# Attention in a one-core Trainium2 kernel: the product of weights and values two steps behind the scores instead of one

## The chip, the cores and the metric

The kernel runs on one core of a Trainium2 chip. The metric is the device time of one execution in microseconds (us); the median of 3 runs is given, and each profile is that of one execution.

## What is computed

The reference is two blocks of layers on 1024 tokens of width 1024. The first is a hybrid mixer with a feed-forward part; the change doesn't touch it. The second has two layers: one with causal attention over 12 heads and one with a linear recurrence, and both with an attention over 256 memory tokens with 4 heads. What matters here:

```
def causal_attention(q, k, v):            # 12 heads, 1024 tokens, q and k 96 wide, v 64 wide
    scale = 1.0 / math.sqrt(d)
    sc = einsum('bqhd,bkhd->bhqk', q_blk, k) * scale
    sc = where(k_pos <= q_pos, sc, -inf)
    p = softmax(sc, axis=-1)
    return einsum('bhqk,bkhd->bqhd', p, v)

def memory_attention(q, mem_k, mem_v):    # 4 heads of 64, 256 memory tokens
    sc = einsum('bshd,bmhd->bhsm', q, mem_k) / math.sqrt(HEAD_DIM)
    p = softmax(sc, axis=-1)
    return einsum('bhsm,bmhd->bshd', p, mem_v)
```

## The kernel before

The kernel is written with explicit semaphores. Each engine has its own list of instructions and runs it in order; where data passes from one engine to another, the reader waits for a count. The function `attention` (from line 3325) is used twice: for the token attention (`causal`, U = 12 heads) and for the memory attention of the second layer (U = 4 heads). The memory attention of the first layer is other code and isn't touched.

The scores are kept transposed: keys on the partitions, queries along the row. A step is one block of 128 keys (`s`) against one half of the queries, 512 of them (`t`). A head u of the token attention has 12 steps: 4 for the first half (t = 0, s = 0 to 3), 8 for the second (t = 1, s = 0 to 7). Blocks on the diagonal and right of it are shorter, 512, 384, 256 and 128 queries, and get a mask product. `mine` is the list of a head's steps. In the memory attention a head has 4 steps, two for each half, all of 512 queries.

For each step n:

- TensorE forms the scores (line 3557, f32, two passes), called S(n) here, into one of two PSUM banks, `ps[:, 4 + n % 2]`. It first waits until the exponential of step n-2 has read that bank (line 3555). On the diagonal a mask product follows (line 3561).
- ScalarE takes the exponential into one of four buffers `pr[:, n % 4]` (line 3602), after the product of step n-4 has read that buffer.
- TensorE multiplies the values with these weights (`weigh(n)`, lines 3482 to 3492, f32, two passes), called W(n), accumulated over the steps of a half in bank 6 + t. It waits for the exponential of step n. The values carry columns of ones, so the sums of the weights come out with it.
- After the last step of a half, VectorE takes the reciprocal of the sums and multiplies (`normalise`, lines 3635 and 3636). It waits for W of that half's last step: W(3) for the first half, W(11) for the second.

To subtract a maximum, the kernel forms for the next head, u + 1, ahead of time the scores a second time in rounded form (`maxima(u + 1, b)`, b = 0 to 7, lines 3508 and 3511), called M(b): each 128 queries against all keys up to them, up to 1024. They go to two pairs of PSUM banks in turn. M(0) waits for the rounded q of that head, which VectorE casts (line 3654); M(b) waits until the content two jobs earlier has been read, which for b from 2 on is the reduction of b-2 on VectorE (`take_maxima`, line 3622). After the eight, `to_rows` (line 3523) turns the maxima by a product with the identity, VectorE negates them (line 3666), and SyncE writes the row to memory and loads it as a 97th row of q by two DMAs (lines 3430 and 3435). The scores of the next head wait for the second DMA.

The order on TensorE around one head: S(0), S(1), the transposition of the next head's values (`turn_values`, line 4197), W(0), then for n from 2: S(n), W(n-1), M(n-2), as long as there are M; at the end `to_rows` and W(11). Then come the projections of K and Q of the head after the next (`project`, line 288 with `latents`), then the next head. On VectorE: reductions 0 and 1, normalise of the first half, reductions 2 to 7, the negated row, normalise of the second half, then rotation and cast of q for the head after the next. ScalarE copies the projections and the values between its exponentials (lines 4202 to 4208). In the memory attention there is nothing between the steps; the maxima of the head after the next follow the head.

Of the kernel before, what the change touches and what calls it, by code (L numbers as in the profile page):

```python
# [157 lines left out]
def build(nc, a):  # L158
    ctx = ExitStack()
    with ctx:  # L160
# [3164 lines left out]
        def attention(iters, U, dq, keys_n, scale, q_of, k_of, v_of, out_of, sfx, rounded, project=None, gating=None):  # L3325
# [61 lines left out]
            with ExitStack() as scope:  # L3387
# [20 lines left out]
                with nc.Block() as block:  # L3408
# [48 lines left out]
                    @block.tensor  # L3457
                    def _(pe):
                        def body(i):
                            reached = {"act": -1, "dve": -1}  # L3460

                            def reads_of(e, value):

                                if value > reached[e]:
                                    reached[e] = value
                                    pe.wait_ge(free[e].sem, val(i, after[e][-1], value))

                            def pair_of(job):

                                j = at[job]  # L3470
                                if j >= 2 or i is not None:
                                    before = (j - 2) % J
                                    for e in readers[jobs[before][0]]:
                                        per = after[e][-1]
                                        value = b_e[e] + after[e][before] - (per if j < 2 else 0)
                                        reads_of(e, value)
                                return pair[j % 2]

                            def evacuated(e, job):
                                reads_of(e, b_e[e] + after[e][at[job]])  # L3480

                            def weigh(n):
                                u, t, s = steps[n]
                                lo, hi = span(t, s)
                                g = 2 * u + t

                                pe.wait_ge(act_p.sem, val(i, len(steps), b_p + n + 1))
                                if s == 0 and (g >= 2 or i is not None):

                                    pe.wait_ge(dve_o.sem, val(i, 2 * U, b_do + g - 1))  # L3490
                                nc.tensor.matmul(ps[:, 6 + t, lo - HALF * t:HALF], v_of(u, s), pr[:, n % 4, 0:hi - lo],  # L3491
                                                 start=(s == 0), stop=(s == last(t))).then_inc(pe_o.sem, 1)

                            def turn_values(u):
                                evacuated("act", ("K", u, 0))
                                project.turn(pair_of(("V", u, 0)))

                            def maxima(u, b):

                                if causal and b == 0:  # L3500
                                    evacuated("act", ("Q", u, 0))
                                    evacuated("dve", ("Q", u, 0))
                                o = pair_of(("A", u, b))
                                if causal:
                                    n_keys = (b + 1) * P
                                    for lo in range(0, n_keys, HALF):
                                        hi = min(lo + HALF, n_keys)
                                        nc.tensor.matmul(o[:, lo:hi], rounded(u)[0][:, b * P:(b + 1) * P],
                                                         rounded(u)[1][:, lo:hi], start=True,
                                                         stop=(hi != n_keys))  # L3510
                                    mm = nc.tensor.matmul(o[:, b * P:n_keys], masks_r[:, 0], masks_r[:, 1],
                                                          start=False, stop=True)
                                else:
                                    for j in range(4):
                                        mm = nc.tensor.matmul(
                                            o[:, j * MEM:(j + 1) * MEM],
                                            rounded(u)[0][:, (4 * b + j) * P:(4 * b + j + 1) * P],
                                            rounded(u)[1], start=True, stop=True)
                                mm.then_inc(pe_done.sem, 1)

                            def to_rows(u):
                                evacuated("dve", ("A", u, CH - 1))
                                nc.tensor.matmul(pair_of(("R", u, 0))[0:CH, 0:P], mx[:, u % 2], ident, start=True,
                                                 stop=True).then_inc(pe_done.sem, 1)

                            for kind, u in seq:
                                if kind == "P":
                                    project(pe, i, u, pair_of, s0)
                                if kind == "V":
                                    turn_values(u)  # L3530
                                if kind == "A":
                                    for b in range(CH if causal else 2):
                                        maxima(u, b)
                                if kind == "R" and causal:
                                    if u == 0:
                                        to_rows(u)
                                elif kind == "R":
                                    evacuated("dve", ("A", u, 1))
                                    o = pair_of(("R", u, 0))
                                    for c in range(CH):  # L3540
                                        mm = nc.tensor.matmul(o[dq:dq + 1, c * P:(c + 1) * P], mx[:, u % 2, c:c + 1],
                                                              ident, start=True, stop=True)
                                    mm.then_inc(pe_done.sem, 1)
                                if kind == "S":
                                    evacuated("dve", ("R", u, 0))
                                    if causal:
                                        evacuated("act", ("V", u, 0))
                                        pe.wait_ge(*row_in.at(16 * (u + 1)))
                                    mine = [n for n, st in enumerate(steps) if st[0] == u]
                                    for n in mine:  # L3550
                                        _, t, s = steps[n]
                                        lo, hi = span(t, s)
                                        if n >= 2 or i is not None:

                                            pe.wait_ge(act_p.sem, val(i, len(steps), b_p + n - 1))
                                        diag = causal and s >= 4 * t
                                        mm = nc.tensor.matmul(ps[:, 4 + n % 2, 0:hi - lo],  # L3557
                                                              k_of(u)[0:dq + 1, s * P:(s + 1) * P],
                                                              q_of(u)[0:dq + 1, lo:hi], start=True, stop=not diag)
                                        if diag:  # L3560
                                            mm = nc.tensor.matmul(ps[:, 4 + n % 2, 0:P], masks_r[:, 0], masks_r[:, 2],  # L3561
                                                                  start=False, stop=True)
                                        mm.then_inc(pe_s.sem, 1)
                                        if causal and u + 1 < U and n - mine[0] == 1:

                                            turn_values(u + 1)
                                        if n > mine[0]:
                                            weigh(n - 1)
                                        if causal and u + 1 < U:
                                            if 2 <= n - mine[0] < 2 + CH:  # L3570
                                                maxima(u + 1, n - mine[0] - 2)
                                    if causal and u + 1 < U:
                                        to_rows(u + 1)
                                    weigh(mine[-1])
                        looped(pe, body)

                    @block.scalar
# [1096 lines left out]
```

## Time and profile before

| | |
|---|---|
| median of 3 runs | 3223.11 us (3221.61 to 3223.95) |
| profiled execution | 3219.17 us, its span 3217.4 us |
| granted TensorE clock, mean over the span | 0.948 |
| TensorE, matmul (PE) | 2929.7 us, 91% |
| VectorE (DVE) | 1504.3 us, 47% |
| ScalarE (ACT) | 1082.7 us, 34% |
| GpSimd (POOL) | 925.9 us, 29% |

The span is what the profiler sees from the first to the last instruction; the execution's own time is a little longer. Busy times of engines overlap. An idle time in a row stands before the instruction it names, with what ended it behind the arrow. The token attention lies at 2323 to 2685 us of the span, the memory attention of the second layer at 3027 to 3086 us.

### The profile page before, as it was taken

Reading aid. Unit: us, or ns where it says so; the run is one execution under the profiler, and the core shown is the slowest. Engines: PE = TensorE matmul, PEld = TensorE weight load, DVE = VectorE, ACT = ScalarE, POOL = GpSimd, SP = SyncE. Lnnn points to the kernel's source line nnn. Section 1 sums busy time; section 2 is a strip of 40 time slices with the busy share of each in tenths; the row PEclk is TensorE's granted clock in tenths of the full one; section 3 lists DMA queues with packets and bytes.
Section 4 is the critical chain, followed back from the end, with each engine's and each line's share of the span. In section 5 each row is a group of like instructions: output and inputs, shape, how many; then the busy total and the mean of one; then the engine's idle time right before and its main releaser. Section 6 shows DMA issues by size and latency. Waiting matters only on the chain. (4 is left out here: it accounts for less than half of the span.)

```text
span 3217.4 us, 34284 instructions
## 1 busy us (share of the span) xinstructions
PE 2929.7 (91%) x14130; PEld 2188.3 (68%) x14130; DVE 1504.3 (47%) x1551; ACT 1082.7 (34%) x1462; POOL 925.9 (29%) x487
## 2 busy tenths in 40 slices
PE   5799999999988889799999999999699998899886
PEld 4677777777766567578887787776455556667565
DVE  4272012243525442565554345343366663639555
ACT  4242122212135123433333444345234341347312
POOL 3241111214332122345544345331112111233110
PEclk8899999999999989899999999999799999899897
DMA  7111124652133352212223453312200001121201
GB/s 291 33 60 53 53 73 149 197 183 79 53 101 123 105 196 62 76 53 79 79 82 102 150 186 122 114 55 73 105 14 20 14 20 72 59 79 33 95 14 53
DMA packets 86173, 286.52 MB, mean 89 GB/s; under 512 B 8849, under 2 KB 13217, under 8 KB 84865
## 3 DMA queue, kind: packets, MB, share of 16 engines
q1 hardware_dynamic: 86018, 284.33, 26.3%
q8 instruction: 112, 1.84, 0.2%
q14 instruction: 43, 0.35, 0.0%
HBM read 219.70 MB, written 64.59 MB: 88 GB/s over the span
## 5 line engine op out<-in xcount | busy, mean ns | idle before, releaser
L280 POOL TENSOR_TENSOR w_lo_sb<-raw_w_sb,w_hi_sb 128x1024 fp32r<-128x1024 f32 x195 | 492.2, 2525 | 1585.0 <-ACT w_hi_sb L271 1584.8
L288 PE MATMUL ps<-h_hi_sb,w_hi_sb 128*128 128x512 f32 x720 | 298.3, 414 | 23.2 <-PEq L910 19.6
L271 ACT ACTIVATE w_hi_sb<-raw_w_sb 128x1024 fp32r<-128x1024 f32 x195 | 205.2, 1052 | 247.9 <-PE ps L288 191.7
L288 PE MATMUL ps<-h_lo_sb,w_hi_sb 128*128 128x512 f32 x720 | 287.5, 399 | 0.0
L288 PE MATMUL ps<-h_hi_sb,w_lo_sb 128*128 128x512 f32 x720 | 244.7, 400 | 0.0
L288 PE MATMUL ps<-merged_parts_hi_sb,w_hi_sb 128*128 128x512 f32 x472 | 192.7, 408 | 18.3 <-PEq L535 7.4
L288 PE MATMUL ps<-z_lo,w_hi_sb 128*128 128x512 f32 x512 | 205.2, 401 | 0.0
L288 PE MATMUL ps<-merged_parts_lo_sb,w_hi_sb 128*128 128x512 f32 x472 | 188.0, 398 | 0.0
L288 PEld LDWEIGHTS ps<-h_hi_sb,w_hi_sb 128*128 128x128 f32 x720 | 137.3, 191 | 67.3 <-issue 34.3
L288 PE MATMUL ps<-merged_parts_hi_sb,w_lo_sb 128*128 128x512 f32 x472 | 178.0, 399 | 0.0
L288 PE MATMUL ps<-z_hi,w_hi_sb 128*128 128x512 f32 x384 | 161.8, 421 | 14.9 <-PEq L910 5.6
L288 PEld LDWEIGHTS ps<-h_hi_sb,w_lo_sb 128*128 128x128 f32 x720 | 137.3, 191 | 33.8
L288 PEld LDWEIGHTS ps<-h_lo_sb,w_hi_sb 128*128 128x128 f32 x720 | 137.5, 191 | 30.6 <-issue 1.0
L288 PE MATMUL ps<-hid_hi_sb,w_hi_sb 128*128 128x512 f32 x352 | 140.5, 399 | 12.9 <-DVE hid_lo_sb L3183 12.9
L3183 DVE TENSOR_TENSOR hid_lo_sb<-ffn_hidden_sb,hid_hi_sb 128x512 fp32r<-128x512 f32 x88 | 85.6, 980 | 127.6 <-ACT hid_hi_sb L3154 127.5
L288 PE MATMUL ps<-hid_lo_sb,w_hi_sb 128*128 128x512 f32 x352 | 140.5, 399 | 0.0
L288 PE MATMUL ps<-hid_hi_sb,w_lo_sb 128*128 128x512 f32 x352 | 139.9, 397 | 0.0
L3557 PE MATMUL ps<-qh_sb,kh_sb 97*128 97x512 f32 (+3 forms) x288 | 123.2, 514 | 13.6 <-DMA qh_sb<-att_rows 11.0
L288 PE MATMUL ps<-z_hi,w_lo_sb 128*128 128x512 f32 x384 | 134.1, 403 | 0.0
L3491 PE MATMUL ps<-att_p_t_sb,vh_sb 128*128 128x512 f32 (+3 forms) x288 | 124.5, 514 | 8.8 <-ACT att_p_t_sb L3602 8.8
L3602 ACT ACTIVATE att_p_t_sb<-ps 128x512 f32<-128x512 f32 (+2 forms) x144 | 69.3, 488 | 175.1 <-PE ps L3561 104.6
L3003 POOL TENSOR_TENSOR w_lo_sb<-ffn_weight_sums_sb,w_hi_sb 128x512 fp32r<-128x512 f32 x72 | 106.8, 1487 | 54.0 <-ACT w_hi_sb L2957 53.7
(627 smaller groups left out, 6391.6 us busy)
## 6 DMA issues: line engine op xcount, KB each, us to landing
raw_w_sb<-in_w SPq DMA_DIRECT2D x231, 512.0 KB, 3.6
ada_late_sb<-in_ada SPq DMA_DIRECT2D x32, 512.0 KB, 3.7
inbox_sb<-gates_out SPq DMA_DIRECT2D x24, 512.0 KB, 4.0
ffn_hidden_out<-ffn_hidden_box_sb SPq DMA_DIRECT2D x22, 512.0 KB, 6.3
ffn_hidden_sb<-ffn_hidden_out SPq DMA_DIRECT2D x22, 512.0 KB, 4.6
ada_w_sb<-in_ada SPq DMA_DIRECT2D x16, 512.0 KB, 8.7
gates_out<-outbox_sb SPq DMA_DIRECT2D x16, 512.0 KB, 2.6
inbox_sb<-sums_out SPq DMA_DIRECT2D x16, 512.0 KB, 4.6
```

Source lines behind the costliest of these rows:

```text
L271: nc.scalar.activation(w_hi[:, n % RING].rearrange("p t m -> p (t m)"), raw_w[:, n % RAW], ACT.Copy).then_inc(w_rounded.sem, 1)
L280: nc.gpsimd.tensor_tensor(w_lo[:, n % RING].rearrange("p t m -> p (t m)"), raw_w[:, n % RAW], flat_hi, ALU.subtract).then_inc(w_split.sem, 1)
L288: mm = nc.tensor.matmul(o, wt, xs, start=start and part == 0 and xs is x_hi, stop=stop and part == 1, skip_group_check=again)
L3003: nc.gpsimd.tensor_tensor(flat4(half_slot(w_lo, j)), weight_of(g, j), flat4(half_slot(w_hi, j)).bitcast(F32), ALU.subtract).then_inc(split ...
L3183: nc.vector.tensor_tensor(hs[1][:, j % RING], source(j), hs[0][:, j % RING].bitcast(F32), ALU.subtract).then_inc(hid_s.sem, 1)
L3491: nc.tensor.matmul(ps[:, 6 + t, lo - HALF * t:HALF], v_of(u, s), pr[:, n % 4, 0:hi - lo], start=(s == 0), stop=(s == last(t))).then_inc(pe ...
L3557: mm = nc.tensor.matmul(ps[:, 4 + n % 2, 0:hi - lo], k_of(u)[0:dq + 1, s * P:(s + 1) * P], q_of(u)[0:dq + 1, lo:hi], start=True, stop=not ...
L3602: nc.scalar.activation(pr[:, n % 4, 0:hi - lo], ps[:, 4 + n % 2, 0:hi - lo], ACT.Exp, scale=scale).then_inc(act_p.sem, 1)
```

## The change

`weigh` of a step stands two steps behind the scores instead of one. Within a head, W(n-2) is issued behind S(n), from the third step on, and both W(n-2) and W(n-1) of the last step follow at the end, behind `to_rows`. It holds for both uses of `attention`. The other engines' lists, the buffers and the waits' conditions are unchanged.

```diff
@@ -3564,13 +3564,14 @@
                                         if causal and u + 1 < U and n - mine[0] == 1:
 
                                             turn_values(u + 1)
-                                        if n > mine[0]:
-                                            weigh(n - 1)
+                                        if n > mine[1]:
+                                            weigh(n - 2)
                                         if causal and u + 1 < U:
                                             if 2 <= n - mine[0] < 2 + CH:
                                                 maxima(u + 1, n - mine[0] - 2)
                                     if causal and u + 1 < U:
                                         to_rows(u + 1)
+                                    weigh(mine[-2])
                                     weigh(mine[-1])
                         looped(pe, body)
```

## Rows read from the trace of the kernel before

**Rows 1.** The page, busy time of each engine, share of the span, instructions.
```profile
PE 2929.7 (91%) x14130; PEld 2188.3 (68%) x14130; DVE 1504.3 (47%) x1551; ACT 1082.7 (34%) x1462; POOL 925.9 (29%) x487
```

**Rows 2.** Grouped by line, PE, 2355 to 2660: busy, mean ns; idle before, releaser.
```profile
L3491 PE MATMUL ps<-att_p_t_sb,vh_sb 128*128 128x512 f32 (+1 forms) x240 | 102.4, 508 | 8.8 <-ACT att_p_t_sb L3602 8.8
...
L3508 PE MATMUL ps<-k_rounded_sb,q_rounded_sb 96*128 96x512 f32 (+2 forms) x120 | 54.5, 508 | 16.3 <-DVE q_rounded_sb L3654 9.6 <-DVE att_max_t_sb L3622 6.6
```

**Rows 3.** Windows, one head: length, busy of each engine, granted clock, DMA share.
```profile
2386.20:2417.40 31.20, 28.68 (x118) 17.13 (x117) 20.73 (x17) 12.79 (x20) 3.04 (x1) 1.00 0.06 18
```

**Rows 4.** Order of time, PE, one head: start, duration, instruction, idle before it.
```profile
2389.80 1.13 PE L3491 MATMUL ps<-att_p_t_sb,vh_sb 128*128 128x512 f32 x2 [0.89 <-ACT att_p_t_sb L3602]
...
2391.26 0.86 PE L3491 MATMUL ps<-att_p_t_sb,vh_sb 128*128 128x384 f32 x2
2393.09 0.30 PE L3508 MATMUL ps<-k_rounded_sb,q_rounded_sb 96*128 96x128 f32 x1 [0.97 <-DVE q_rounded_sb L3654]
...
2395.22 0.39 PE L3491 MATMUL ps<-att_p_t_sb,vh_sb 128*128 128x128 f32 x2
2395.36 0.42 PE L3508 MATMUL ps<-k_rounded_sb,q_rounded_sb 96*128 96x384 f32 x1
...
2395.70 1.08 PE L3557 MATMUL ps<-qh_sb,kh_sb 97*128 97x512 f32 x2
2396.61 1.02 PE L3491 MATMUL ps<-att_p_t_sb,vh_sb 128*128 128x512 f32 x2
...
2397.77 1.08 PE L3557 MATMUL ps<-qh_sb,kh_sb 97*128 97x512 f32 x2
2398.68 1.02 PE L3491 MATMUL ps<-att_p_t_sb,vh_sb 128*128 128x512 f32 x2
2400.37 0.56 PE L3508 MATMUL ps<-k_rounded_sb,q_rounded_sb 96*128 96x512 f32 x2 [0.66 <-DVE att_max_t_sb L3622]
...
2408.15 0.86 PE L3491 MATMUL ps<-att_p_t_sb,vh_sb 128*128 128x384 f32 x2
2408.85 0.39 PE L3557 MATMUL ps<-qh_sb,kh_sb 97*128 97x128 f32 x2
```

**Rows 5.** Order of time, DVE, the same head.
```profile
2390.22 2.73 DVE L3654 CAST q_rounded_sb<-qh_sb 32x1024 fp32r<-32x1024 f32 x1
...
2395.65 3.36 DVE L3635 RECIPROCAL att_rec_t_sb<-ps 64x512 f32<-64x512 f32 x1 [0.71 <-PE ps L3491]
...
2399.76 2.10 DVE L3622 TENSOR_REDUCE att_max_t_sb<-ps 128x1 f32<-128x384 f32 x3
```

**Rows 6.** Order of time, PE, the first scores of the last head.
```profile
2662.40 1.10 PE L3557 MATMUL ps<-qh_sb,kh_sb 97*128 97x512 f32 x2 [2.57 <-issue]
```

**Rows 7.** Order of time, DVE, memory attention: first row of maxima, last head's first reciprocal.
```profile
3042.57 1.22 DVE L3669 TENSOR_SCALAR lru_qm_sb<-ps 1x1024 f32<-1x1024 f32 x1 [0.51 <-PE ps L3541]
...
3077.72 3.35 DVE L3635 RECIPROCAL att_rec_m_sb<-ps 64x512 f32<-64x512 f32 x1 [0.71 <-PE ps L3491]
```

**Rows 8.** Windows, PE alone, 8 us from an idle stretch's start: length, busy, clock, DMA.
```profile
27.50:35.50 8.00, 3.68 (x44) 1.00 0.82 277
187.80:195.80 8.00, 6.17 (x67) 1.00 0.20 68
254.30:262.30 8.00, 6.19 (x58) 0.79 0.20 66
291.40:299.40 8.00, 5.55 (x17) 0.79 0.29 97
...
1362.10:1370.10 8.00, 6.80 (x30) 1.00 0.68 255
...
2154.70:2162.70 8.00, 5.45 (x20) 0.79 0.28 99
2659.80:2667.80 8.00, 5.43 (x14) 0.79 0.01 2
```

## The prediction

> **What bounds the kernel now.** I read the page first: TensorE (PE) is busy 91% of the span, so a wait of PE costs time and a wait of another engine does not [rows 1]. Then I grouped the instructions by line over the ten full heads of the token attention, 2355 to 2660 us. That shows where PE stands still and who ends it: 8.8 us ahead of the products with the values, ended by ScalarE's exponentials; and 16.3 us ahead of the score products for the maxima of the next head, all of it ended by VectorE (DVE), 9.6 us by its cast of the rounded q and 6.6 us by its reduction [rows 2]. One head takes 31.2 us at a granted clock of 1.00 [rows 3]. Last I read one head in order of time, PE beside DVE. I call a score product S, the product of weights and values W, a product for the maxima of the next head M. A head has S0 to S11, W0 to W11 and M0 to M7. The order before is S(n), W(n-1), M(n-2).
>
> The reader should see three stops of PE in each head [rows 4]: 0.89 us ahead of W0, 0.97 us ahead of M0, 0.66 us ahead of M4; the rest is back to back. M0 waits for DVE's cast, which starts at 2390.22 and takes 2.73 us: it ends at 2392.95, M0 starts at 2393.09. M4 waits for the third reduction. DVE works through a fixed list: reductions 0 and 1, then the reciprocal and the product of the head's first half, then reductions 2 to 7. The reciprocal waits for W3, the last product of the first half; it starts at 2395.65, takes 3.36 us, and the reductions start at 2399.76 [rows 5]. From the start of the reciprocal to M4 it is 2400.37 - 2395.65 = 4.72 us. So in this part of the head the path runs W3, reciprocal, product, reduction, M4, and PE fills only a part of it with M2, S5, W4, M3, S6, W5.
>
> **What the change moves.** W(n-2) stands behind S(n), and the last two W stand at the head's end, behind the transposition of the maxima. No instruction is added or removed, on any engine, and no DMA. What each move costs, in order:
>
> *The stop ahead of W0.* W0 waits for exponential 0. In the new order S2 stands first, but S2 writes the buffer that exponential 0 reads, so it waits for the same event. The 0.89 us stay. The gain that the change seems to offer, cover for the exponentials, is already there in the rest of the head: no other W of the full heads shows an idle PE, since 8.8 us is ten heads by 0.88 [rows 2]. I cost the gain at nothing; what hides the exponential at present is the S that stands between.
>
> *The stop ahead of M0.* Its end is set by DVE's cast and stays. W1 ran in front of it (2391.26) and now runs behind M0, behind S3. It has 384 columns; such a W takes 2408.85 - 2408.15 = 0.70 us [rows 4]. So the stop grows from 0.97 to about 1.67 us.
>
> *W3, and DVE behind it.* Between M0 and W3 there now stand also W1 (0.70), M2 (at most 2395.70 - 2395.36 = 0.34 us; I take 0.3) and S5 (2396.61 - 2395.70 = 0.91) [rows 4]. W3 ends 1.9 us later. What waits in DVE's list behind it is the reciprocal and, queued behind that, all reductions from 2 on, and PE waits for reduction 2 at M4. M4 starts 1.9 us later.
>
> *The stop ahead of M4.* W5 (0.9 us, as S5; it has the same 512 columns) was done before M4 and is now done after it. So M4 comes 1.9 us later with 0.9 us less behind it: 2.8 us a head. Check from the other side: between W3 and M4 PE loses M2, S5 and W5 of its filling, 0.3 + 0.91 + 0.9 = 2.1 us, so this stop grows from 0.66 to about 2.8 us; with 0.70 at M0 that is 2.8 again. Behind M4 PE is back to back, before and after, so nothing is won back.
>
> *Count.* Ten heads have both stops: 28 us. The first head, which lies ahead of that stretch, finds its cast long done and has no stop ahead of M0, but the same list of DVE: 2.1 us. The twelfth has no M. Together 30.1 us. The bounds: 2.5 a head if M2 costs nothing, 3.1 if each of the moved products leaves a tenth of a us more between itself and its neighbour than the rows show; 27 to 33 us.
>
> *The end of a head.* The transposition of the maxima stands ahead of W10 now, so the row of maxima leaves for its two DMAs about 0.5 us earlier (W10 has 256 columns, against 0.70 us for 384). Those DMAs are hidden behind the projections of the head after the next, except for the last head, where PE stops 2.57 us [rows 6]: -0.5 us. The queue of SyncE is moved past nothing else; GpSimd waits for the second half's product only, whose place stays.
>
> *Memory attention.* Four heads of four steps. W1 now stands behind S3, about 0.9 us later, and DVE's reciprocal behind it. In the first and third head DVE stood only 0.51 us idle before the next head's row of maxima [rows 7], so 0.4 us each comes through; in the last head the chain from 3077.72 on is DVE's alone, two reciprocals and two products, and the next stage waits for it: 0.9 us. Together +1.7 us. Less than nothing here would need a stop at the last W, and PE shows none to speak of; more would need the half clock, so 0 to 4 us.
>
> Sum without the clock: 30.1 - 0.5 + 1.7 = 31.3 us.
>
> **The clock.** A stop of PE can also cost speed afterwards. In this trace I looked up the single idle stretches of PE inside dense work and the granted clock over the 8 us from their start [rows 8]. With about 1.2 us idle (8 less 6.80 busy) the clock stays at 1.00. With about 1.8 us it stays once (187.80) and falls once (254.30); over all six stretches between 1.76 and 1.96 us three were followed by a fall. With 2.2 to 2.6 us (291.40, 2154.70, 2659.80 and two more) it fell in five of six; the sixth (27.50) kept 1.00. A mean of 0.79 over 8 us is 8 x 0.21 = 1.7 us of full-speed work lost, at the lower of the two levels, 1.2 instead of 2.4 GHz, until the clock rose again. The new stop ahead of M4, 2.8 us, is at or above the longest of these, so I take 5/6 x 11 heads x 1.7 = 15.6 us. The stop ahead of M0 becomes 1.67 us with the 0.89 us one close before it; its nearest rows are those at 1.8 us. I take one head in three: 3.4 x 1.7 = 5.8 us. Bounds: nothing, or 21 falls by 1.7 = 36 us. I take 21.4 us, since the rows at 2.5 us are the nearest to the larger stop.
>
> The Trainium skill ("TensorE: Matmul & The Clock Gate", section "HAM oscillation — how this bites in real kernels") warns only of idle gaps longer than the two reckoned here. By that rule no head would lose any clock and the time would be that of the rival without the clock, below; the trace does not agree, since 2.5 us was enough for it five times.
>
> Sum: 31.3 + 21.4 = 52.7 us. The profiled execution has a span of 3217.4 and a time of 3219.17 us, so it would take 3271.9; it lies 3.9 us under the median of the three runs, 3223.11, and from that the sum gives 3275.8. I say 3274.
>
> **Rivals.**
> *The stops without the clock.* Only the M0 and M4 mechanism: 3223.1 + 27 to 38 = 3250 to 3261. For it: two gaps of 0.89 and 0.97 us in every head left the clock at 1.00 [rows 3], and one of 2.2 us did. Against it: rows 8.
> *The clock falls at both stops in every head.* 31.3 + 36 = 67, and a few falls that last twice as long: 3287 to 3305. For it: the two stops ahead of M0 add to 2.5 us within some 4 us. Against it: the stop at M0 alone, 1.67 us, is shorter than any after which the clock fell.
> *Faster.* The place is the wait of W0 for exponential 0: if it went into the cover of S2, and the stop at M4 were set by the buffers rather than by DVE's list, ten heads would gain 0.88, some 9 us: 3214. The point from which it decides: exponential 0 has to be done before S2's turn, and reduction 2 has to start before W3 ends. Neither the list of DVE nor S2's buffer allows it.
> *Nothing changes.* The two orders would be worth the same if PE's stops merely changed places: 3217 to 3229. It would need M4 not to wait for W3's reciprocal; the 0.66 us in each head say it does.
>
> **Chances.** The forecast with clock (3262 to 3286) 0.50; without clock 0.20; both stops 0.20; some other slower way, such as memory attention at half clock throughout, 0.02; faster 0.04; no change 0.04. The range has to take in most of the first three: I reach down to 3248, below the case without clock, and up to 3294, half of the case with both. That leaves out about 0.18. What a measurement of this kernel can tell from no change is about 0.2%, 6.4 us. Faster 0.04, within 0.04, slower 0.92.
>
> **What would show it.** In the changed kernel's page DVE stays at 1504 us of busy time and PE's grows only by what runs at half clock. Grouped by line over the same ten heads, the idle time ahead of the maxima's score products grows from 16.3 to about 45 us, some 28 of it ended by DVE's reduction and 16 to 17 by the cast; the 8.8 us that ScalarE ends stay, but stand ahead of S2. In order of time the reciprocal starts 1.9 us later after M0. The granted clock in a head's stretch falls to between 0.90 and 0.97. I am wrong if M4's stop stays near 0.7 us (then DVE was not what it waits for), or if it is 2.8 us and the clock stays at 1.00 (then only the step on the clock fails).

## The result and the profile after

The changed kernel takes 3295.99 us (median of 6 runs, 3285.35 to 3297.74), the kernel before in the same series 3222.36 (6 runs, 3217.72 to 3227.60). The ratio is 1.022, with a 95% interval of 1.021 to 1.023: slower by 2.2%, 73.6 us by the medians. The forecast was 3274 us, 1.6%. The ratio applied to the 3223.11 us from which the forecast was made gives 3294.3, at the very top of its range of 3248 to 3294; the median itself lies 2 us above it. One execution below, the profiled one of the first filling experiment, was disturbed as a whole (12811.73 us) and is left out of that kernel's time.

The profiled execution has a span of 3294.3 us, 76.9 more than before. The work is the same, PE's busy time is longer. First the page, busy time of each engine, against [rows 1]:

```profile
PE 2976.1 (90%) x14130; PEld 2210.9 (67%) x14130; DVE 1503.7 (46%) x1551; ACT 1082.7 (33%) x1462; POOL 925.1 (28%) x487
```

Where the time came from, by stretches of the span. From the kernel before, the token attention and the memory attention (length; busy of PE, its weight loads, DVE, ACT, POOL; granted clock; DMA share, GB/s):

```profile
2322.80:2681.40 358.60, 329.67 (x1302) 193.86 (x1302) 226.01 (x186) 137.28 (x222) 60.88 (x22) 0.99 0.05 15
3031.60:3086.50 54.90, 45.85 (x130) 20.13 (x128) 42.53 (x26) 9.55 (x16) 0.00 (x0) 0.82 0.02 7
```

The same two of the changed kernel:

```profile
2327.80:2754.60 426.80, 369.41 (x1302) 211.51 (x1302) 226.15 (x186) 137.19 (x222) 60.88 (x22) 0.89 0.04 13
3104.80:3163.60 58.80, 47.09 (x130) 21.10 (x128) 42.55 (x26) 9.55 (x16) 0.00 (x0) 0.80 0.01 5
```

The token attention is 68.2 us longer, the memory attention 3.9. The remaining 5 us lie ahead of both, in code that the change doesn't touch. That part ends at 2322.8 us before, at 2327.8 after, and in the experiments below between 2320.7 and 2335; so it differs from one execution to the next, and I draw nothing from it. I compare stretches and heads within the attention. Heads 1 to 9 take 31.16 to 31.17 us from start to start in the kernel before, and 31.14 to 31.19 in an execution of another kernel below that keeps their order.

PE grouped by line over the ten full heads of the changed kernel (2363 to 2736 us; busy, mean ns; idle before, releaser), against [rows 2]:

```profile
L3557 PE MATMUL ps<-qh_sb,kh_sb 97*128 97x512 f32 (+1 forms) x243 | 122.1, 592 | 11.1 <-ACT att_p_t_sb L3603 8.8 <-issue 2.3
L3491 PE MATMUL ps<-att_p_t_sb,vh_sb 128*128 128x512 f32 (+1 forms) x240 | 114.1, 567 | 0.0
L3508 PE MATMUL ps<-k_rounded_sb,q_rounded_sb 96*128 96x512 f32 (+2 forms) x120 | 65.6, 605 | 43.0 <-DVE att_max_t_sb L3623 26.8 <-DVE q_rounded_sb L3655 16.1
```

The 8.8 us that ScalarE's exponentials end stand now ahead of the scores instead of the product with the values, and are the same 8.8. The idle time ahead of the maxima's products grew from 16.3 to 43.0 us. And the means grew: 567 ns for the product with the values where [rows 2] has 508. That is the clock, as the stretches below show.

One head in order of time, PE (start, duration, instruction, idle before it), against [rows 4]:

```profile
2367.28 0.70 PE L3557 MATMUL ps<-qh_sb,kh_sb 97*128 97x256 f32 x2 [0.89 <-ACT att_p_t_sb L3603]
...
2370.56 0.30 PE L3508 MATMUL ps<-k_rounded_sb,q_rounded_sb 96*128 96x128 f32 x1 [1.61 <-DVE q_rounded_sb L3655]
...
2372.00 1.91 PE L3557 MATMUL ps<-qh_sb,kh_sb 97*128 97x512 f32 x2
...
2376.18 0.39 PE L3491 MATMUL ps<-att_p_t_sb,vh_sb 128*128 128x128 f32 x2
...
2381.33 0.56 PE L3508 MATMUL ps<-k_rounded_sb,q_rounded_sb 96*128 96x512 f32 x2 [2.69 <-DVE att_max_t_sb L3623]
...
2383.07 1.91 PE L3491 MATMUL ps<-att_p_t_sb,vh_sb 128*128 128x512 f32 x2
```

And DVE beside it, against [rows 5]:

```profile
2367.69 2.72 DVE L3655 CAST q_rounded_sb<-qh_sb 32x1024 fp32r<-32x1024 f32 x1
...
2376.60 3.35 DVE L3636 RECIPROCAL att_rec_t_sb<-ps 64x512 f32<-64x512 f32 x1 [3.98 <-PE ps L3491]
...
2380.72 2.11 DVE L3623 TENSOR_REDUCE att_max_t_sb<-ps 128x1 f32<-128x384 f32 x3
...
2412.11 3.36 DVE L3636 RECIPROCAL att_rec_t_sb<-ps 64x512 f32<-64x512 f32 x1 [2.30 <-PE ps L3491]
```

The reader should see three things. The three stops are 0.89, 1.61 and 2.69 us where they were 0.89, 0.97 and 0.66. DVE stands idle 3.98 us ahead of the reciprocal, waiting for W3, where it stood 0.71: the late W3 starts the chain late, and the chain itself is unchanged, 2376.60 to 2381.33 = 4.73 us (4.72 before). Part of the 3.98 us is the low clock between M0 and W3. The last row is of the next head, where the clock stayed up behind M0 at 2407.74: there DVE stands idle 2.30 us, and the reciprocal starts 4.37 us behind M0 where it started 2.56 before, so 1.8 us later by the order alone. And a score product of 512 columns behind the stop at M0 and a value product behind the one at M4 take 1.91 us, where they take 1.0 to 1.1 at full clock (a row marked x2 is the two passes together).

The granted clock, heads 1 to 3 of the changed kernel as stretches, against [rows 3]:

```profile
2363.60:2400.80 37.20, 32.01 (x118) 18.61 (x117) 20.73 (x17) 11.83 (x19) 10.50 (x4) 0.91 0.04 15
2400.80:2437.80 37.00, 31.82 (x117) 18.46 (x117) 20.72 (x17) 12.78 (x20) 3.04 (x1) 0.91 0.05 15
2437.80:2476.20 38.40, 33.22 (x118) 19.25 (x117) 20.73 (x17) 11.83 (x19) 8.20 (x3) 0.87 0.04 15
```

Eight us from the start of a stop, PE alone, as in [rows 8]: first three at M4, then two at M0:

```profile
2378.60:2386.60 8.00, 5.31 (x14) 0.79 0.01 3
2415.80:2423.80 8.00, 6.97 (x14) 0.57 0.01 2
2454.60:2462.60 8.00, 5.95 (x16) 0.79 0.00 0
2368.90:2376.90 8.00, 6.39 (x23) 0.79 0.18 66
2406.10:2414.10 8.00, 6.38 (x26) 1.00 0.24 66
```

In the trace the lower level comes with the stop at M4 in eleven heads of eleven, in three of them for twice as long (0.57), and with the stop at M0 in seven of ten, three of them twice as long. It starts between 0.9 us before the stop's end and 1.8 us after it.

### The profile page after: what moved, and what is told of

Its sections match the earlier page's. It is cut to its first block and busy times, and to the rows that moved or that the text cites. A ratio compares the mean times of both kernels' runs of the same rounds, so it can differ in the third digit from the quotient of the medians.

```text
span 3294.3 us, 34284 instructions
## 1 busy us (share of the span) xinstructions
PE 2976.1 (90%) x14130; PEld 2210.9 (67%) x14130; DVE 1503.7 (46%) x1551; ACT 1082.7 (33%) x1462; POOL 925.1 (28%) x487
## 5 line engine op out<-in xcount | busy, mean ns | idle before, releaser
L3557 PE MATMUL ps<-qh_sb,kh_sb 97*128 97x512 f32 (+3 forms) x288 | 144.4, 591 | 22.0 <-DMA qh_sb<-att_rows 10.9
L3491 PE MATMUL ps<-att_p_t_sb,vh_sb 128*128 128x512 f32 (+3 forms) x288 | 135.9, 564 | 0.0
L3508 PE MATMUL ps<-k_rounded_sb,q_rounded_sb 96*128 96x512 f32 (+2 forms) x144 | 78.1, 604 | 51.4 <-DVE att_max_t_sb L3623 29.5
```

The costliest lines, as they stand in the source:

```text
L3557: mm = nc.tensor.matmul(ps[:, 4 + n % 2, 0:hi - lo], k_of(u)[0:dq + 1, s * P:(s + 1) * P], q_of(u)[0:dq + 1, lo:hi], start=True, stop=not ...
```

## The experiments

Two prices were to be told apart: the waiting of PE, and the speed it loses after it. Then their causes: DVE's list for M4, the position of W3, the order itself. The code is shortened: `...` stands for lines and indices that are left out. Each kernel's ratio is to the kernel before, run in the same series.

**Filling the stop ahead of M4 with useless work.**

```diff
+for _ in range(10 if b == 3 and u else 0):
+    nc.tensor.matmul(o[:, 0:HALF], rounded(u)[0][:, b * P:(b + 1) * P],
+                     rounded(u)[1][:, 0:HALF], start=True, stop=True)
```

> The changed kernel with more work: in each of eleven heads ten more products of 512 columns, copies of the first product of M3 with the same operands and the same place, stand in front of it, and so in the stop ahead of M4. They take about 2.2 us and end before VectorE's third reduction, so they move no other instruction. Theory (two prices, the stops and the clock that falls after them): time falls although work is added, by the clock that was lost behind the eleven stops at M4, some 15 to 25 us, to 3270 to 3282 us; the granted clock falls only behind the stops at M0. Rival (the clock fell for another reason, or its loss lay under other waits; the 73 us are all in the order of the products): 3296 or more. The output is unchanged.

Measured: 3266.17 us (median of three), ratio to the kernel before 1.012 (1.011 to 1.014), against 1.022 for the changed kernel. Adding 110 products made it faster, by about 1% of the time and by 4 us more than the range expected. For a profile of it there is one more execution:

> The kernel that fills the stop ahead of M4 with ten copies of M3's first product, once more, for its profile (the profiled execution of the first run of it was disturbed as a whole). Theory: behind M4 the clock no longer falls in any head; behind M0 it still falls in six or seven of ten, so that heads of 33.8 us alternate with heads of about 36 us, and the whole comes to 3262 to 3275 us. Rival (falls at M4 are not due to the idle time): falls behind M4 stay. The output is unchanged.

Measured: 3271.73 us. Grouped by line over its ten full heads (idle before, releaser):

```profile
L3511 PE MATMUL ps<-k_rounded_sb,q_rounded_sb 96*128 96x512 f32 (+2 forms) x120 | 55.2, 514 | 20.1 <-DVE q_rounded_sb L3658 16.1 <-DVE att_max_t_sb L3626 3.9
L3507 PE MATMUL ps<-k_rounded_sb,q_rounded_sb 96*128 96x512 f32 x100 | 25.4, 400 | 0.0
```

PE waits for the reduction 3.9 us in place of 26.8, since the copies stand in the stop. Behind M4 the clock falls in no head; behind M0 in four. The heads without a fall take 33.8 us, the others 35.5 to 37.0. I had expected the falls at M0 in six or seven; the rest is as the theory says.

**Filling both stops.**

```diff
+if causal and 0 < u < U - 1 and t == 0 and s == 0:
+    nc.tensor.matmul(ps[:, 6 + t, ...], v_of(u, s), pr[:, n % 4, ...], start=True, stop=True)
```

> As the one before, and W0 of ten heads is formed twice, once more in the stop ahead of M0, which leaves about 0.75 us of its 1.61. Theory: no head loses clock any more and what is left is the waiting alone, 30 us for the heads and 2 to 4 for the memory attention, so 3223 + 32 = 3255 us, 3250 to 3260, with a granted clock of 1.00 in the heads' stretches. Rival (the clock's loss is small and the order costs more than the 2.8 us a head reckoned): 3285 or more. The output is unchanged.

Here the filling ahead of M3 is in too. Measured: 3256.33 us, ratio 1.009 (1.008 to 1.011). Its heads as stretches:

```profile
2364.00:2397.80 33.80, 31.75 (x130) 19.28 (x128) 20.70 (x18) 11.80 (x20) 10.51 (x4) 1.00 0.05 16
2397.80:2431.60 33.80, 31.79 (x130) 19.29 (x128) 20.71 (x18) 12.76 (x21) 3.04 (x1) 1.00 0.06 16
```

From start to start heads 1 to 9 take 33.81 to 33.85 us at full clock: 31.17 + 2.66. The copies stand inside the stops, of which 0.76 us at M0 and 0.4 at M4 are left. So the waiting alone costs 2.66 us a head. The heads of the changed kernel take 37.0 to 38.4 (the first 35.9), so the clock costs a further 3.1 to 4.6 us a head. It is the larger part of the 73 us.

**DVE's list in another order.** The changed order on TensorE, reductions 2 and 3 ahead of the reciprocal:

```diff
-between = range(2) if causal and u + 1 < U else ()
+between = range(4) if causal and u + 1 < U else ()
...
-for b in range(2, CH):
+for b in range(4, CH):
```

> The changed order on TensorE, but VectorE takes the reductions 2 and 3 ahead of the first half's reciprocal instead of behind it. If M4 waits for nothing but VectorE's list, its stop of 2.7 us (and the 0.66 of before) is gone and with it its fall of the clock; left are the stop at M0, 1.61 instead of 0.97, seven us in all, and its share of the clock, 12 to 20 us, and the memory attention: 3223 + 7 - 7 + 4 + 16 = 3243 us, 3232 to 3252. If W3 or the order itself is what costs, the time stays at 3285 or more. The output is unchanged.

Measured: 3256.84 us, ratio 1.010 (1.008 to 1.011). Ten heads by line, and two as stretches:

```profile
L3508 PE MATMUL ps<-k_rounded_sb,q_rounded_sb 96*128 96x512 f32 (+2 forms) x120 | 64.6, 593 | 16.2 <-DVE q_rounded_sb L3655 16.2
...
2366.00:2400.10 34.10, 31.60 (x118) 19.00 (x117) 20.73 (x17) 11.89 (x20) 10.50 (x4) 0.90 0.05 16
2400.10:2434.20 34.10, 31.60 (x117) 18.89 (x116) 20.80 (x18) 12.86 (x21) 3.04 (x1) 0.90 0.05 16
```

The mechanism is shown: PE waits for no reduction any more, neither the 26.8 nor the 6.6 us of before. The size was missed: 3243 us was expected, 3252 at most. The stop at M0 was followed by a fall of the clock not in seven heads of ten but in every one, and each time for 6.8 us. To see that this is all that the heads' 34.1 us hold, the stop at M0 was filled in this kernel too, by W0 formed twice:

```diff
+if causal and 0 < u < U - 1 and t == 0 and s == 0:
+    nc.tensor.matmul(ps[:, 6 + t, ...], v_of(u, s), pr[:, n % 4, ...], start=True, stop=True)
```

> The kernel with the changed order and VectorE's reductions 2 and 3 moved ahead (its heads took 34.1 us, 3.0 more than before, though it waits no longer than before in sum), with W0 of ten heads formed twice, so that the stop ahead of M0 shrinks from 1.62 to about 0.75 us and nothing else moves. Theory (the 3.0 us are the clock, which fell for 6.8 us behind M0 in every head): the heads take 31.2 us, with more work in them, and the granted clock is 1.00. Rival (they are waits or the order of the products): 34 us or more. The output is unchanged.

Measured: 3215.43 us in one execution. One head:

```profile
2351.00:2381.90 30.90, 29.26 (x120) 17.58 (x119) 20.73 (x17) 11.83 (x19) 10.51 (x4) 1.00 0.06 18
```

30.9 us, not even the 31.2 of the kernel before: one repeated product of 0.9 us, put into a stop of which 0.76 us stay, took 3.2 us off each head. The loss after a stop of 1.62 us was twice as long as the stop.

**W3 in its old place.** With the changed order W3 follows W2 behind S4:

```diff
+early = causal and u + 1 < U
-if n > mine[1]:
+if n > mine[1] and not (early and n == mine[5]):
     weigh(n - 2)
+if early and n == mine[4]:
+    weigh(n - 1)
```

> The changed order, except that W3 of each head follows W2 behind S4, its old place, so VectorE's reciprocal starts earlier; from S6 on the distance is two again. Theory by the sum's steps: W3 ends 0.7 us later than before (by W1 alone) instead of 1.9; the stop at M0 stays 1.61, the one at M4 is 0.66 + 0.9 (W5) = 1.5 to 1.6 instead of 2.69; a head takes 31.2 + 0.7 + 0.9 = 32.8 us without a fall of the clock and up to 3.4 more with it. Rival (it isn't W3 that VectorE's list and M4 wait for): the stop at M4 stays at 2.7. The output is unchanged.

Measured: 3258.06 us in one execution. Ten heads by line, a head without and one with a fall:

```profile
L3508 PE MATMUL ps<-k_rounded_sb,q_rounded_sb 96*128 96x512 f32 (+2 forms) x120 | 59.3, 548 | 30.9 <-DVE q_rounded_sb L3658 16.1 <-DVE att_max_t_sb L3626 14.9
...
2360.60:2393.30 32.70, 28.68 (x118) 17.12 (x117) 20.73 (x17) 11.84 (x19) 10.52 (x4) 1.00 0.05 17
2393.30:2428.80 35.50, 31.51 (x118) 18.78 (x117) 20.72 (x17) 12.78 (x20) 3.04 (x1) 0.90 0.05 16
```

The stop at M4 is 1.5 us, as the sum's steps give, and the head 32.67 us against 32.8 forecast. Heads with and without a fall alternate, and a fall costs 2.86 us. So W3's place is a cause: back in it, the stop at M4 is 1.2 us shorter, of the 2.66 us a head that the waiting costs. It isn't the only one. The other 1.5 us stay, and by the sum's steps they are W1, now behind M0 (0.7), and W5, now behind M4 (0.9).

**The memory attention alone.** The token attention keeps its order.

```diff
-if n > mine[0]:
+if causal and n > mine[0]:
     weigh(n - 1)
+if not causal and n > mine[1]:
+    weigh(n - 2)
...
+if not causal:
+    weigh(mine[-2])
 weigh(mine[-1])
```

> The change in the memory attention alone; the token attention keeps the order of before. Theory: the last head's first reciprocal waits for W1, which now stands behind S3: 1.7 us more by VectorE's chain, up to 4 with the clock, so 3223 to 3228 us, and the stretch from the first score product of memory to the next stage's first product grows from 54.9 by 1.5 to 4 us. Rival (the memory attention gains, since its exponentials have more cover): that stretch gets shorter. The token attention's heads stay at 31.2 us either way. The output is unchanged.

Measured: 3237.03 us in one execution, more than expected. The heads of the token attention stayed at 31.14 to 31.19 us, the first at 31.33. From the first score product of memory to the next stage's first product it is 60.2 us, against 54.9; but the untouched part ahead of the attention took 10 us more than in the profile of before, and this one execution can't be read as a whole. Over the kernels with this change in them the stretch is 58.8 or 60.2 to 60.4 us, without it 53.2 to 54.9, so it costs at least 3.9 us, above the 1.7 of the sum. The next stage's first product waits 7.27 us in the changed kernel and 6.31 before, first row below. The second is the stretch of this kernel, whose granted clock is 0.76:

```profile
3163.70 0.77 PE L288 MATMUL ps<-z_hi_sb,w_hi_sb 128*128 128x512 f32 x1 [7.27 <-PEq L3408]
...
3043.50:3103.70 60.20, 48.66 (x129) 21.72 (x129) 42.54 (x26) 9.55 (x16) 0.00 (x0) 0.76 0.01 5
```

What the clock takes can be estimated from the stretches: 54.9 x 0.18 = 9.9 us of full-speed work before, 58.8 x 0.20 = 11.8 in the changed kernel, 60.2 x 0.24 = 14.4 here. That is 1.9 of its 3.9 us and 4.5 of these 5.3, so most of what varies from kernel to kernel is the clock. No kernel here separates the two by filling a stop.

**A better order.** If both stops come from M's place, M should come later. The order of before, W one step behind S, with M0 and M1 behind S4 and W3, then one a step:

```diff
-if 2 <= n - mine[0] < 2 + CH:
-    maxima(u + 1, n - mine[0] - 2)
+for b in {4: (0, 1)}.get(n - mine[0], (n - mine[0] - 3,)):
+    if n - mine[0] >= 4 and b < CH:
+        maxima(u + 1, b)
```

> The order of before (W one step behind S), with the maxima's products later: M0 and M1 behind S4 and W3, then one a step. S3, W2, S4 and W3, some 2.0 us, fill the 0.97 us ahead of M0, and the reciprocal no longer stands in front of M4 with too little work: from M1 to M4 there are 5.9 us of work for the 4.7 of VectorE's chain. Theory: both stops go, 0.97 + 0.66 = 1.6 us a head, heads of 29.5 us and 3225 - 17 = 3208 us. Rival (the stops only move to another place, such as the product that turns the maxima): 3220 to 3230. The output is unchanged.

Measured: 3207.59 us, ratio 0.995 (0.993 to 0.996). By line PE waits for neither the cast nor a reduction ahead of these products, and heads take 29.6 us:

```profile
L3508 PE MATMUL ps<-k_rounded_sb,q_rounded_sb 96*128 96x512 f32 (+2 forms) x114 | 54.7, 542 | 0.0
```

Then ScalarE's rounding of the next weights, moved behind the fourth exponential:

```diff
+if u < 2:
     round_slot(act, i, s0 + u + RING, U)
...
+if causal and 0 < u < U - 1 and n == step_at[(u, 0, 3)]:
+    round_slot(act, i, s0 + u + 1 + RING, U)
```

> As the one before, and ScalarE rounds the next weights (1.05 us) behind the fourth exponential of a head instead of in front of the first. Exponential 0 starts some 0.9 us earlier and the stop of 0.89 us ahead of W0 goes. Theory: 0.8 us a head more, heads of 28.7 us, 3199 us. Rival (W0 waits for something else, or the later rounding holds up the weights of a later head): 3208 or more. The output is unchanged.

Measured: 3200.49 us, ratio 0.992 (0.991 to 0.993), faster than both kernels of this study. The stop ahead of W0 is gone, heads take 28.65 us. What is left is a stop ahead of the product that turns the maxima, since M7 and its reduction now come late:

```profile
2410.48 0.39 PE L3523 MATMUL ps<-cst_sb,att_max_t_sb 128*8 128x128 f32 x2 [0.50 <-DVE att_max_t_sb L3626]
```

**The change on top of the better order.**

```diff
-if n > mine[0]:
-    weigh(n - 1)
+if n > mine[1]:
+    weigh(n - 2)
...
+weigh(mine[-2])
 weigh(mine[-1])
```

> The change under study laid on the kernel with the late maxima and the late rounding (3200 us, heads of 28.65 us). There VectorE's list has room: from W3 to M4 there are M2, S6, W4, M3, S7 and W5, 4.2 us of work for the 4.7 us of its chain, so the stop at M4 is about 0.5 us; at the head's end one product more covers the last reduction, -0.2 us. Theory (the change costs what it takes from the cover of VectorE's chain, and nothing else): heads of 28.9 to 29.2 us, no fall of the clock in them, and with 4 us for the memory attention 3206 to 3213 us. Rival (two steps' distance costs 2.7 us a head in itself): heads of 31.3 us, 3234 us or more. The output is unchanged.

Measured: 3210.36 us, ratio to the kernel before 0.995 (0.993 to 0.997). One head:

```profile
2364.30:2393.70 29.40, 28.45 (x118) 17.23 (x117) 18.60 (x17) 11.84 (x19) 9.38 (x4) 1.00 0.07 19
...
2377.17 0.56 PE L3508 MATMUL ps<-k_rounded_sb,q_rounded_sb 96*128 96x512 f32 x2 [0.67 <-DVE att_max_t_sb L3627]
```

29.36 us, 0.7 more than the 28.65 below it (0.2 to 0.5 were expected), at full clock. The stop at M4 is back with 0.67 us, the one ahead of the product that turns the maxima fell from 0.50 to 0.28, and 0.25 us of the 0.7 shows in no wait. The two kernels' times were taken in different series and their ratios' intervals touch (0.993), so the heads are the proof here and not the times. The same edit that costs 5.8 to 7.2 us in each of heads 1 to 9 of the kernel before costs 0.7 where the chain behind W3 has more cover.

## Why the prediction was right, point by point

- *The stop ahead of W0 stays.* Right: 8.8 us before, 8.8 us after, now ahead of S2. Nothing was gained by the cover.
- *The stop ahead of M0, 0.97 to 1.67.* Right: 1.61.
- *W3 1.9 us later, M4 with it, its stop 0.66 to 2.8.* Right: 1.8 us at full clock, the stop 2.69, with the chain from the reciprocal to M4 unchanged. The sum was 2.8 us a head; filled to full clock the heads show 2.66. That DVE's list is the cause is shown by the kernel with the reductions ahead, and that W3's place sets 1.2 us of it by the kernel with W3 early. Under "What would show it" the reciprocal was to start 1.9 us later after M0 in every head; where the clock falls at M0 it is 3.5.
- *The end of a head, -0.5.* The right way, but 0.3: the last head's stop is 2.25 us, from 2.57.
- *Memory, 1.7 in 0 to 4.* Too small: 3.9 in the profile, up to 5.5 in the others. The wait at its end grew by 0.96, near the 0.9 reckoned; the clock was left out of the value.
- *The clock, 21.4.* This term was mis-sized. The token attention grew by 68.2 us; ten heads by 2.66 and the first by 2.0 are 28.6 of it, so the clock cost about 40. I took 5/6 of eleven falls at M4 and a third of ten at M0 (as 3.4, it is 3.3), each of 1.7 us. The trace has eleven and seven, six of them twice as long: 14 times 1.7 us at M4, where 15.6 us stood, and 10 times at M0, where 5.8 stood. For M0 the step that failed is the count: I looked at 1.67 us alone, with its nearest rows at 1.8 us, and set the 0.89 us stop close in front of it aside. The trace of before holds a nearer case that I overlooked, so it isn't true that no fall followed a stop as short as 1.67 us. It has 1.62 and 0.95 us idle, 1.45 us from the end of the one to the end of the other, and then the lower level:

```profile
1118.82 0.50 PE L2398 MATMUL ps<-ml_rows_sb,ml_selx_sb 36*128 36x512 f32 x1 [1.62 <-DVE ml_rows_sb L2588]
...
1120.27 0.50 PE L288 MATMUL ps<-y_parts_hi_sb,w_hi_sb 128*128 128x512 f32 x1 [0.95 <-DVE outbox_b_sb L1351]
...
1117.20:1125.20 8.00, 5.43 (x13) 0.79 0.16 66
```

The length I took from single stops in work without such stops, where one fall in eight or so was long; here, in heads that repeat, a third of them were.
- *The number.* Without the clock the sum was right: 31.3 us, and the kernel with both stops filled takes 30.7 more than the kernel before in its series (3225.68). The result is the time of the rival in which the clock falls at both stops, 3287 to 3305, with a chance of 0.20. The range reaches it only because it was stretched half-way into that rival; that it just sufficed is luck.
- *The rival without the clock*, which the rule of the Trainium skill ("TensorE: Matmul & The Clock Gate", section "HAM oscillation — how this bites in real kernels") would give, fell: stops of 2.69 and even 1.62 us were followed by the lower level, and the kernel without these falls, 3256 us, had to be made by filling them.

## What to carry to other kernels

Before a consumer is moved back in an in-order queue, look for what waits for its last instance and what stands in that engine's list behind the waiter. Here all value products but W0 had the cover they needed, and one of them, W3, started a chain of 4.7 us on another engine that PE waited for. Look also at what the move takes out from in front of an existing wait: W1 at M0 and W5 at M4 made up the rest. A stop of PE has two prices. In these loops a stop of 1.6 us was followed by a fall of the clock in four to ten passes of ten, and one of 2.7 us in all eleven, so the upper bound of a forecast should count one fall for each pass, with neighbouring stops looked at together. And work moved into such a stop can be worth more than its own time: here even repeated products that nobody needs took the kernel from 3296 to 3256 us.

## What the runs showed of the hardware

Three things I had not expected. First, the falls recur in step with the loop: with heads of 34.1 us every head fell, for 6.8 us each, and in the kernel with W3 early heads of 32.67 and 35.5 us took turns. The same stop of 1.61 us cost nothing in some heads and 1.7 to 3.2 us in others. It suggests that the length of everything around a stop decides, and that a small change elsewhere can switch the fall on for all passes; no run varied that length by itself.

Next, how long a fall lasts goes with when it starts. The changed kernel, PE alone, around the stop at M4 that ends at 2381.33 and the one that ends at 2416.83:

```profile
2375.60:2381.30 5.70, 3.04 (x10) 1.00 0.00 1
2382.40:2385.70 3.30, 3.30 (x8) 0.50 0.02 5
2414.20:2416.40 2.20, 0.00 (x0) 1.00 0.00 0
2416.50:2423.30 6.80, 6.47 (x12) 0.50 0.01 2
2423.40:2430.00 6.60, 6.60 (x27) 1.00 0.00 1
```

The first fall starts behind the stop and lasts 3.4 us, the second starts while PE still stands and lasts 6.8. So it is with all 37 falls at M0 and M4 in the four profiles that have any (the changed kernel, the filled M4, the reductions ahead, W3 early): the 23 that start before the stop has ended last 6.8 us, the 14 others 3.4. Elsewhere it doesn't always hold: ahead of the last head of the kernel with both stops filled, a fall that starts 0.5 us behind the stop lasts 6.8.

Last, DVE's cast of q, 32x1024, takes 2.71 to 2.73 us in every head of the kernels before and after, with GpSimd's split of the weights running beside it. In the kernel with the late rounding GpSimd works later, and the same cast takes 0.68 us in the full heads. From that kernel, DVE and then GpSimd (nothing ran on GpSimd between 2389.2 and 2396.06):

```profile
2393.49 0.68 DVE L3658 CAST q_rounded_sb<-qh_sb 32x1024 fp32r<-32x1024 f32 x1
2396.06 2.35 POOL L280 TENSOR_TENSOR w_lo_sb<-raw_w_sb,w_hi_sb 128x1024 fp32r<-128x1024 f32 x1 [6.83 <-ACT w_hi_sb L271]
```

GpSimd's own instruction takes 2.35 us there instead of 3.04. So the stop ahead of M0, the one that the change made longer and that cost a clock fall in seven heads, rests on a cast that takes four times as long as when alone. In both kernels each cast ends 0.55 us behind that GpSimd instruction, as it would if it were held until then; whether it is held or slowed, the runs can't tell. All this was seen, not tried by itself; moving only GpSimd's part would be the next experiment.
